# Sparse attention branch: two heads of a channel tile per step, on halves of TensorE's array, with fp32 values and turned probabilities

## The reference

```
logits = einsum('bqhd,bqkd->bhqk', qb, ks) * scale
logits = logits - slopes[None, :, None, None] * dist[:, None]
logits = jnp.where(valid[:, None], logits, -jnp.inf)
p = jax.nn.softmax(logits, axis=-1)
out = einsum('bhqk,bqkd->bqhd', p, vs)
```

## Time and profile before

| | us |
|---|---|
| median of 3 runs | 1546.64 (1543.2 to 1550.14) |
| the profiled execution's own time | 1545.01 |
| its span | 1543.1 |
| phase c, window attention | 208 to 480 |
| phase a, forgetting attention | 722 to 961 |
| phase b, sparse attention | 961 to 1266 |
| TensorE busy | 1454.7 (94%) |
| VectorE busy | 774.1 (50%) |
| ScalarE busy | 704.4 (46%) |

### The profile page before, as it was taken

How to read it: one execution, slowest core, us unless ns; L and a number is a source line. 1 busy time by engine, 2 the same in 40 slices (tenths; PEclk the granted TensorE clock), 3 DMA queues, 4 the chain that set the end, 5 groups by cost and what they waited for, 6 DMA issues and landing times.

```text
span 1543.1 us, 21545 instructions
## 1 busy us (share of the span) xinstructions
PE 1454.7 (94%) x8082; PEld 1161.3 (75%) x8082; DVE 774.1 (50%) x1665; ACT 704.4 (46%) x1530; POOL 67.0 (4%) x142
## 2 busy tenths in 40 slices
PE   4978899999999999999999999999999999999898
PEld 3766577777776778887777767788888878888786
DVE  5354855544555984464433334654445446232533
ACT  6354766666765551112555555454444442211412
POOL 1102300000000000000000000000000000000000
PEclk8998999999999999999999999999999999999999
DMA  5115521111111112222100101312222221222322
GB/s 172 31 32 137 126 52 35 35 28 35 34 42 28 41 39 62 75 76 86 28 24 25 29 15 33 126 42 62 69 69 88 63 76 48 62 75 89 126 103 99
DMA packets 111513, 97.17 MB, mean 63 GB/s; under 512 B 10673, under 2 KB 98097, under 8 KB 111153
## 3 DMA queue, kind: packets, MB, share of 16 engines
q1 hardware_dynamic: 100816, 58.54, 14.2%
q0 software_dynamic: 10592, 37.23, 7.8%
HBM read 73.21 MB, written 18.35 MB: 59 GB/s over the span
## 4 chain that ended last, share of the span: by engine, by line
PE 79%; DVE 4%; ACT 2%; issue 1%; ACTq 0%; DVEq 0%; DMA 0%; POOL 0%; POOLq 0%
PE bank L788 20%; PE bank L790 20%; PE bank L789 20%; PE bank L956 6%; PE bank L983 4%; PE slot L943 2%; PE slot L933 2%; PE slot L788 1%; PE slot L919 1%; PE slot L789 1%; PE slot L918 1%; PE slot L790 1%; DVE idle_out L1400 1%; ACT pta L1250 1%; PE bank L892 1%
## 5 line engine op out<-in xcount | busy, mean ns | idle before, releaser
L788 PE MATMUL bank<-hs,w_hl 128*128 128x512 f32 x1152 | 464.6, 403 | 9.2 <-DVE tm L1659 5.1
L790 PE MATMUL bank<-hs,w_hl 128*128 128x512 f32 x1152 | 453.8, 394 | 0.0
L789 PE MATMUL bank<-hs,w_hl 128*128 128x512 f32 x1152 | 453.5, 394 | 0.0
L788 PEld LDWEIGHTS bank<-hs,w_hl 128*128 128x128 f32 x1152 | 219.7, 191 | 54.7 <-issue 8.6
L790 PEld LDWEIGHTS bank<-hs,w_hl 128*128 128x128 f32 x1152 | 218.8, 190 | 48.1
L1373 DVE TENSOR_TENSOR w_hl<-w_raw,w_hl 128x512 fp32r<-128x512 f32 (+1 forms) x176 | 118.9, 679 | 270.5 <-ACT w_hl L1074 268.2
L789 PEld LDWEIGHTS bank<-hs,w_hl 128*128 128x128 f32 x1152 | 219.9, 191 | 43.7 <-issue 0.8
L1074 ACT ACTIVATE w_hl<-w_raw 128x512 fp32r<-128x512 f32 (+1 forms) x176 | 109.1, 622 | 187.3 <-PE bank L790 184.0
L1573 DVE TENSOR_TENSOR ptb<-bank,ptb 128x512 fp32r<-128x512 f32 (+2 forms) x96 | 50.6, 555 | 134.5 <-ACT ptb L1247 134.5
L1400 DVE TENSOR_SCALAR_CACHE_REDUCE idle_out<-score,state 128x768 uint8<-128x768 f32 (+3 forms) x140 | 115.3, 824 | 4.8
L1265 ACT ACTIVATE yb<-bank 64x128 f32<-64x128 f32 x64 | 17.2, 269 | 140.8 <-PE bank L790 140.8
(11 more groups left out here) (306 smaller groups left out, 2379.8 us busy)
## 6 DMA issues: line engine op xcount, KB each, us to landing
w_raw<-in_w_in_dram SPq DMA_DIRECT2D x142, 256.0 KB, 2.8
merged_scratch<-ms POOLq DMA_DIRECT2D x16, 512.0 KB, 3.3
ms<-merged_scratch POOLq DMA_DIRECT2D x16, 512.0 KB, 4.0
xn<-in_x_dram SPq DMA_DIRECT2D x8, 512.0 KB, 6.9
iq_st<-iq_hl POOLq DMA_DIRECT2D x32, 128.0 KB, 3.4
qb<-qb_scratch POOLq DMA_DIRECT2D x8, 512.0 KB, 4.1
w_raw<-in_w_o_dram SPq DMA_DIRECT2D x16, 256.0 KB, 3.7
qb_scratch<-bq_high POOLq DMA_DIRECT2D x8, 256.0 KB, 3.5
```

What stands on the lines that cost most here:

```text
L788: pe.matmul(out_, wh, mh, start=start, stop=False)
L789: pe.matmul(out_, wh, ml, start=False, stop=False)
L790: return pe.matmul(out_, wl, mh, start=False, stop=stop)
```

## The change

In phase b a unit becomes two heads of a channel tile, with `pair_run` in place of `softmax_run`: 32 units and 34 steps, filler at 2 x 0.84 pieces a step. Logits become three products per head on 64 rows, values become one fp32 product per chunk and head on 64 columns, both heads reading the same values tile. The turned probabilities are copied once by ScalarE, into four buffers. The low parts of v and of the probabilities go, with their VectorE steps and one load. q is kept in DRAM by channel tile and part, spilled by two DMAs of 512 KB per tile, and loaded in halves of 512 columns.

```diff
-PTS = {"a": 4, "b": 2, "c": 4}
+RATE_B = 0.84
+PTS = 4
...
-    softmax_run([dict(br="b", ch=h // 2, hh=h % 2, b=b, W=(b + 1) * P, h=h)
-                 for h in range(B_HEADS) for b in range(TB)], {}, 0.89)
+    pair_run([dict(br="b", ch=ch, b=b, W=(b + 1) * P) for ch in range(NCH["b"]) for b in range(TB)], {}, RATE_B)
...
-                    for part in range(2):
-                        for hh in range(2):
-                            pool.dma_start(qb_dram[2 * a["c"] + hh, HD * part:HD * part + HD, :],
-                                           bq_hl[part][HD * hh:HD * hh + HD, :]).then_inc(q_spilled, 16)
+                    for part in range(2):
+                        pool.dma_start(qb_dram[a["c"], part], bq_hl[part][:]).then_inc(q_spilled, 16)
...
+            def load_q(ch, half):
+                src = qb_dram[ch].rearrange("t p x -> p t x")[:, :, half * HALF:(half + 1) * HALF]
+                pool.dma_start(qb[:, half], src).then_inc(qb_in[half], 16)
...
-                        for c0 in range(0, W, HALF):
-                            c1 = min(W, c0 + HALF)
-                            pe.matmul(o[:, c0:c1], q, khb[:, 0, c0:c1], start=True, stop=False)
-                            ins = pe.matmul(o[:, c0:c1], q, khb[:, 1, c0:c1], start=False, stop=True)
...
+                            tq = slice(a["b"] % 4 * P, (a["b"] % 4 + 1) * P)
+                            qt, kt = qb[:, a["b"] // 4, :, tq], khb
                         for c0 in range(0, W, HALF):
                             c1 = min(W, c0 + HALF)
                             for n, (qp, kp) in enumerate(((0, 0), (0, 1), (1, 0))):
                                 for hh in range(2):
                                     rows = slice(HD * hh, HD * hh + HD)
-                                    ins = pe.matmul(slot_of(a, hh)[1][:, c0:c1], qt[rows, qp, tq], kt[rows, kp, c0:c1],
+                                    ins = pe.matmul(slot_of(a, hh)[1][:, c0:c1], qt[rows, qp, :], kt[rows, kp, c0:c1],
                                                     start=n == 0, stop=n == 2)
...
-                                ins = split_product(o, V["b"][:, c, :], vb_low[:, c, :], pt[:, 0, j, :], pt[:, 1, j, :],
-                                                    c == 0, c == n - 1)
...
+                            values = V["b"][:, c, :] if a["br"] == "b" else V[a["br"]][a["ch"] % 2][:, first + c, cols]
+                            ins = pe.matmul(bank[a["pv"][0]][cols, 0:P], values, PT[a["br"]][:, t, j, :],
+                                            start=c == 0, stop=c == n - 1)
...
-                            v.tensor_tensor(lo, bank[b][:, 0:n * P], hi.bitcast(F32), ALU.subtract).then_inc(bank_free[b], 1)
```

More of the change, by code:

```diff
@@ L165, in flush @@
         flush_later()
[L167 to L196, removed]
     picking = [("bit", n) for n in range(32)] + [("bound", 0), ("above", 0), ("above", 1), ("count", 0), ("equal", 0), ("equal", 1)]
@@ L608, in last_slot @@
         def last_slot(u):
-            return u["S"] + u.get("slots", 1) - 1
+            return u["S"] + u["slots"] - 1
         steps = {}
@@ L761, in _ @@
                                        src[:, q % 2, :]).then_inc(iq_in[a["h"] % 2], 16)
[L762 to L767, removed]
+                elif kind == "logits" and a["br"] == "b" and a["b"] in (0, 4):
+                    ch, half = a["ch"], a["b"] // 4
+                    if ch == half == 0:
+                        load_q(0, 0)
+                        load_q(0, 1)
                         load_first_sums(1)
+                    elif ch + half < NCH["b"]:
+                        pool.wait_ge(slot_full, a["S"])
+                        load_q(ch + half, 1 - half)
                 elif kind == "w" and a["th"]:
@@ L950, in _ @@
                         claim(pe, grp["use"])
[L951 to L955 removed]
+                        for j, (row, c) in enumerate(grp["parts"]):
                             ins = pe.transpose(bank[grp["use"][0]][:, j * P:(j + 1) * P],
@@ L1228, in _ @@
                 elif kind == "exp":
-                    back = 2 if a["br"] == "b" else 1
-                    if a["unit"] >= back:
-                        full(act, units[a["unit"] - back]["groups"][-1]["use"])
-                    for hh in heads(a):
-                        act.wait_ge(logit_ready, logit_of(a, hh) + 1)
+                    if a["unit"]:
+                        full(act, units[a["unit"] - 1]["groups"][-1]["use"])
+                    for hh in range(2):
+                        act.wait_ge(logit_ready, a["L"] + hh + 1)
                         mx, dn = stats_of(a, hh)
-                        row = a["unit"] % 2 if a["br"] == "b" else hh
-                        ins = A(PR[a["br"]][:, row, 0:a["W"]], slot_of(a, hh)[1], ACTF.Exp, bias=mx, scale=-1.0, accum_out=dn)
-                        if hh == heads(a)[-1] or a["slots"] == 2:
+                        ins = A(PR[a["br"]][:, hh, 0:a["W"]], slot_of(a, hh)[1], ACTF.Exp, bias=mx, scale=-1.0, accum_out=dn)
+                        if hh or a["slots"] == 2:
                             ins.then_inc(slot_free, 1)
@@ L1255, in _ @@
                     full(act, a["pv"])
[L1256 to L1259 removed]
+                    y, src = Y[br][:, ch, :], bank[a["pv"][0]][:, 0:P]
                     if br == "c" and ch // 2 == 2:
@@ L1552, in _ @@
                 elif kind == "logits":
-                    slope = 2.0 ** (-(a["h"] + 1)) if a["br"] == "b" else 1.0
-                    for hh in heads(a):
+                    for hh in range(2):
+                        slope = 2.0 ** (-(2 * a["ch"] + hh + 1)) if a["br"] == "b" else 1.0
                         s, o = slot_of(a, hh)
```

107 lines of the change are left out of this document (30 added, 77 removed).

## The result

The changed kernel took 1523.54 us (median of 4 runs, 1519.37 to 1528.18), the kernel before 1545.72 on the same chip: ratio 0.9852, 95% interval 0.9831 to 0.9873. The forecast was 1524, the range 1515 to 1536.

What follows compares the result with a forecast made beforehand. TensorE's instruction stream was taken to bound the sparse stage. 19.5 us less there and 2.5 in the index stage took 22 off 1545.01, giving 1523, stated as 1524 because the runs' median is 1.6 higher; range 1515 to 1536.

Steps and rivals of the forecast that it cites:

- The forgetting stage as a measurement of the new code: Sparse stage: the forgetting stage's units already have the new form and price it; 294.2 us becomes 274.7.
- A tile's attention: Sparse stage, per channel tile: logits, values and turns without projection pieces take 26.7 us, against 32.1 before.
- The filler: Sparse stage: all 57 projection pieces fit, one or two per step, at 2.83 us instead of 2.76, costing 4.0 us.
- Waits in the first dozen steps: Start of the sparse stage: the merge's z reads queue ahead of the next logits; 5 us of waits, bounds 0 and 14.
- five shares: Sparse stage: five share products of about 0.3 us each stay, 1.6 us.
- Rival B: Sparse values: one shared tile makes the halves run in turn, 0.48 us per chunk, not 0.24; 1558 us, chance 0.04.
- Rival A: Wide sparse steps: logits wait for both exponentials of the step before; 1534 us in part (0.14), 1546 in full (0.05).
- The relief of VectorE: Sparse stage: VectorE's low part of the turned probabilities goes, and with it TensorE's 6.2 us of waits for it.
- Spill: Index stage: two q spill DMAs per tile instead of four shorten ScalarE's waits; 2.5 us less, between 0 and 4.7.
- Sum: Whole kernel: 19.5 us from the sparse stage and 2.5 from the index stage, 22 us off.

Runs made afterwards that it cites:

- fp32 kernel: Kernel before, one head at a time, with sparse values as one fp32 product per chunk and head and no low parts: 1563.4 us, ratio 1.011.

## Why the prediction was right

- **The forgetting stage as a measurement of the new code.** Right to 2%. A tile's attention was to be 26.7 us. The two tiles read are 63.98 - 13 x 2.83 = 27.2 and 66.74 - 14 x 2.83 = 27.1; logits, values and turns came out at the very 1.60, 1.68 and 2.24.
- **The filler.** All 57 pieces fit, two in a row at 5.65 us, single ones mostly at 2.84 to 2.94. Together they take 162.5 us, 2.85 each where 2.83 was taken, 4.9 us more than before where 4.0 was forecast. The reason given was partly wrong: the prediction laid the longer piece to its place in the step and read it as a change of tiling mode. But a piece and the turns beside it are both on the full array (128x128). The fp32 kernel shows the same cost at the old place, from an fp32 neighbour; ahead of the 64-row logits a piece's last product also takes 0.32 us and not 0.23.
- **Waits in the first dozen steps.** Taken at 5 us, measured about 1.5: 272.96 less 4 x 27.15, 57 x 2.83 and five shares at 0.3. They were two waits in one step, 0.6 and 0.9, at the merge's reads. This 3.5 and the tiles' 1.8 are the two mis-sized terms; together they give 273.0 for the 274.7 forecast.
- **Rival B** was the right thing to fear: values by head show that without overlap almost nothing is left of the gain (ratio 0.9978). Its other part, that one shared tile would prevent the overlap, is false: 1.90 us for eight chunks.
- **Rival A** did not occur, because each wide step has a piece; with the pieces gone it costs 11.5 us in waits.
- **The relief of VectorE.** It was credited with waits alone, and that is right: TensorE's idle time in the stage fell by 3.6 us, and by 5.5 in the fp32 kernel. The rest of the stage's 21.3 needs the halves: with values by head the stage gives back 19.6, with the logits on one half 25.6.
- **Spill.** 2.5 forecast, 2.1 measured twice.
- **Sum.** 23.4 us by the stages, 22.2 by the medians, 22 forecast. That the two last agree so well is partly luck: the errors of the terms cancel in part, and the repeat of the same two kernels has 1547.53 - 1520.92 = 26.6.

## What to carry to other kernels

If another stage of the same kernel already runs the form that a change brings, take its period from the starts of two repeats, take off the pieces, and price the change by that, not by busy sums. Fp32 in place of three rounded products, for values of 128x64 by 128 columns, paid here only where two products ran on separate halves of the array, so put neighbours on different halves, or in runs of no more than four records (two fp32 products). And keep independent work between a step's turns and its values: it hid the softmax chain here, and where it had run out the clock fell to 0.94.

## What the runs showed of the hardware that was not expected

- The two halves of the array's rows run apart from each other: three products of 64 rows on one half and three on the other take as long as alternating ones (1.60 us for twelve of 512 columns), six and six take 2.16, all on one half 2.95.
- Products start out of the program's order across the halves. In threes the other half's first, fourth in the list, starts within 0.01 us of the list's first; in longer runs it starts when three records of the first half have still to start.
- For fp32 products on column halves a run of two is free (0.59 us for two chunks in either order), runs of four cost 0.48 to 0.60 more, of eight 1.36 more.
- A unit of fp32 products pays about 0.15 us once, which the rounded ones (1.26 us for 21) don't show, and the piece ahead of it pays 0.09.
- At the same point of the changed kernel, TensorE busy 16.74 of 20 us, the granted clock was 1.00 in one execution and 0.83 in another. The spans of these two differ by 9.6 us (1526.2 and 1516.6) and their sparse stages by 0.01, so compare stages and not spans.
